# A hybrid encoder layer on eight cores: norms before the adaLN products, weights in 4 KB rows, the gate summed on VectorE, two buffers for normalized x

## The reference

```
mod = silu(c) @ w_ada + b_ada                     # (B, 3D)
shift, scale, gate = split(mod, 3)
h = rmsnorm(x, norm_g) * (1 + scale) + shift
a, ga, u, v, gb, ma, mb = split(h @ w_in, ...)    # 5 x 512, 2 x 1024 columns
y_a = (real 2-D DFT of a over (positions, 128 channels), mixed per group) * silu(ga)
y_b = (u * (w_s mixing layernorm(v) in chunks of 128 positions)) * silu(gb)
merged = sigmoid(ma) * (y_a @ w_pa) + sigmoid(mb) * (y_b @ w_pb)
y = rmsnorm(x + gate * (merged @ w_out), final_g)
```

## Time and profile before

| | |
|---|---|
| median of 3 runs | 1419.55 us (1417.86 to 1419.67) |
| profiled execution, its own time | 1415.01 us |
| its span on the slowest core (4); the others | 1413.5 us; 1406.5 to 1413.1 |
| granted TensorE clock, mean of each core | 0.953 to 0.959 |
| busy, core 4: TensorE, VectorE, ScalarE, GpSimd | 1245.9, 585.4, 503.5, 321.7 us |
| DMA | 48503 packets, 149.84 MB, 106 GB/s in the mean |

### The profile page before, as it was taken

How to read it: one execution, slowest core, us unless ns; L and a number is a source line. 1 busy time by engine, 2 the same in 40 slices (tenths; PEclk the granted TensorE clock), 3 DMA queues, 4 the chain that set the end, 5 groups by cost and what they waited for, 6 DMA issues and landing times.

```text
span 1413.5 us, 19855 instructions; the slowest of 8 cores (1406.5 to 1413.5 us)
## 1 busy us (share of the span) xinstructions
PE 1245.9 (88%) x6412; PEld 601.3 (43%) x6524; DVE 585.4 (41%) x956; ACT 503.5 (36%) x875; POOL 321.7 (23%) x398
## 2 busy tenths in 40 slices
PE   6476299699999997777996999999999699999997
PEld 1243144344444444443543444444444344444443
DVE  0353123344344445665433433444334334444344
ACT  0562213143332436664431334323343233333321
POOL 0000014413032130000145131321313613223122
PEclk9698699899999999999998999999999899999999
DMA  9899952122121255653521221212215112212111
GB/s 285 227 198 170 216 129 90 45 90 90 45 76 60 90 177 172 200 164 109 159 66 45 90 90 45 76 60 90 90 61 135 60 46 75 89 61 91 45 75 60
DMA packets 48503, 149.84 MB, mean 106 GB/s; under 512 B 5772, under 2 KB 18444, under 8 KB 45074
## 3 DMA queue, kind: packets, MB, share of 16 engines
q1 hardware_dynamic: 44514, 122.20, 25.4%
q0 software_dynamic: 2592, 17.96, 7.9%
q10 hardware_dynamic: 1296, 8.40, 1.9%
HBM read 135.03 MB, written 31.47 MB: 118 GB/s over the span
## 4 chain that ended last, share of the span: by engine, by line
PE 76%; DMA 8%; DVE 4%; issue 4%; ACT 4%; POOL 2%; SPq 1%; ACTq 0%; DVEq 0%; POOLq 0%
PE ps L652 41%; PE ps L610 12%; PE ps L743 6%; PE ps L737 6%; DMA Gd<-arena 5%; PE ps L662 5%; PE ps L498 2%; DMA arena<-w_ada 2%; ACT arena L442 2%; POOL arena L647 2%; PE ps L466 2%; ACT arena L479 1%; PE ps L820 1%; DMA arena<-Gd 1%; DVE arena L448 1%
## 5 line engine op out<-in xcount | busy, mean ns | idle before, releaser
L652 PE MATMUL ps<-arena 128*128 128x512 bf16 x2634 | 596.2, 380 | 7.1 <-DVE arena L692 3.7
L652 PEld LDWEIGHTS ps<-arena 128*128 128x128 bf16 x2688 | 262.4, 98 | 319.7 <-issue 8.0
L610 PE MATMUL ps<-arena 128*128 128x512 bf16 x734 | 173.9, 389 | 42.8 <-POOL arena L647 32.0
L729 ACT ACTIVATE arena<-ps 128x512 bf16<-128x512 f32 x192 | 113.2, 597 | 263.2 <-PE ps L652 259.7
L748 POOL TENSOR_TENSOR arena<-arena 128x512 bf16<-128x512 bf16 x96 | 125.1, 1303 | 283.3 <-DVE arena L746 283.3
L740 DVE TENSOR_TENSOR arena<-ps,arena 128x512 bf16<-128x512 f32 x96 | 66.4, 692 | 254.5 <-PE ps L737 254.5
L615 DVE TENSOR_TENSOR arena<-ps,arena 128x512 f32<-128x512 f32 x96 | 66.0, 691 | 189.7 <-PE ps L610 189.7
L610 PEld LDWEIGHTS ps<-arena 128*128 128x128 bf16 x768 | 75.9, 100 | 133.9 <-issue 50.1
L618 ACT ACTIVATE arena<-arena 128x1024 bf16<-128x1024 f32 x48 | 50.7, 1057 | 179.0 <-DVE arena L615 179.0
L442 ACT ACTIVATE arena<-arena 128x1024 bf16<-128x1024 f32 x96 | 100.5, 1047 | 6.1 <-DMA arena<-xB 5.9
L737 PE MATMUL ps<-arena 128*128 128x512 bf16 x384 | 98.6, 379 | 0.0
(11 more groups left out here) (79 smaller groups left out, 948.7 us busy)
## 6 DMA issues: line engine op xcount, KB each, us to landing
arena<-xB SPq DMA_DIRECT2D x96, 512.0 KB, 4.0
arena<-xA SPq DMA_DIRECT2D x48, 512.0 KB, 5.1
yu<-arena SPq DMA_DIRECT2D x48, 512.0 KB, 2.8
arena<-w_in POOLq DMA_DIRECT2D x9, 1024.0 KB, 19.4
arena<-w_ada ACTq DMA_DIRECT2D x8, 1024.0 KB, 19.7
Gd<-arena SPq DMA_DIRECT2D x48, 128.0 KB, 2.6
arena<-Gd SPq DMA_DIRECT2D x12, 512.0 KB, 6.9
arena<-w_out POOLq DMA_DIRECT2D x6, 1024.0 KB, 12.8
```

What stands on the lines that cost most here:

```text
L610: S.pe([lambda e, b=b, dmc=dmc, half=half: e.matmul(ps[b][:], lhsT=mg[:, dmc, j * 128:(j + 1) * 128], rhs=w_out_sb[:, dmc, half * 512:(hal ...
L652: S.pe([lambda e, kc=kc: e.matmul(ps[b][:], lhsT=w_in_sb[:, sec, kc, col:col + 128], rhs=hT0[:, kc, :], start=(kc == 0), stop=(kc == 7)) f ...
L729: S.op("act", lambda e, b=b, so=so: e.activation(out=bv(so, 512), in_=ps[b][:], func=AF.Sigmoid), reads=[("ps", b)], writes=gk(so, 1024))
```

## The change

Six things. (1) The norms: groups 0 and 1 of the first block are squared and scaled before the adaLN rows are copied out; the transposes of group 0 (`fe_t`) stand between the fifth and sixth piece of the adaLN products, the evictions with Gtab and modT (`fe_e`) after them. SP loads four chunks, the tables, and four more once the seventh piece of w_ada is there. (2) The weights lie in DRAM as blocks of 128 rows of 1024 float32, so that each partition's 16 KB come in four rows of 4 KB. (3) Normalized chunks have two buffers (`xoffs`), used by turns; the unused output of the squares goes to O_TYB. The ring of x chunks in A2 has 6 places instead of 8. (4) In both blocks chunks are normed in pairs: two squares, one root, one reciprocal, then the first chunk's scale on VectorE and the second's on GpSimd. (5) The gate: for each unit, `gate_acc` on VectorE multiplies each of the eight pieces with the condition's value per partition and adds them up, `gate_sum` sums over the partitions with a product with ones (float32, two of 512 columns) and adds the bias; gate_d and the three-row products are gone. The eight pieces and the bias are now loaded for each of the three units. (6) `gate_mul` runs on VectorE, and from other merge steps.

```diff
-    w_in = din("w_in", [9 * 128, 4096])
-    w_pa = din("w_pa", [128, 4096])
-    w_pb = din("w_pb", [128, 4096])
-    w_out = din("w_out", [128, 8192])
+    w_in = din("w_in", [9 * 512, 1024])
+    w_pa = din("w_pa", [512, 1024])
+    w_pb = din("w_pb", [512, 1024])
+    w_out = din("w_out", [1024, 1024])
...
+    def blocks(t, k):
+        return dram_ap(t, k * 512 * 1024, [[1024, 128], [128 * 1024, 4], [1, 1024]])
+
     def w_sec(s, after=()):
-        S.dma("pool", [lambda e: e.dma_start(
-            out=bv(O_WIN + 8192 * s, 4096), in_=w_in.ap()[s * 128:(s + 1) * 128, :])],
-            "s_w%d" % s, reads=after, writes=wink[s])
+        S.dma("pool", [lambda e: e.dma_start(out=bv(O_WIN + 8192 * s, 4096).rearrange("p (k n) -> p k n", k=4),
+                                             in_=blocks(w_in, s))], "s_w%d" % s, reads=after, writes=wink[s])
...
-    def x_sq(k, j, mode="pow"):
-        si = st_ctr[0] % 8
-        st_ctr[0] += 1
-        xk, sk = gk(XS[k], 4096), gk(O_XSR + 2048 * j, 2048)
-        S.op("act", lambda e: e.activation(out=xsr[:, j, :], in_=fv(XS[k], 1024), func=AF.Square, scale=0.03125,
-                                           accum_out=stat[:, si, 0:1]),
-             reads=xk, writes=sk + [("st", si)])
-        rstd(1, stat[:, si, 0:1], stat[:, si, 1:2], [("st", si)], [("st1", si)], mode)
-
-        def scale():
-            S.op("dve", lambda e: e.tensor_scalar(out=xsr[:, j, :], in0=fv(XS[k], 1024), scalar1=stat[:, si, 1:2],
-                                                  scalar2=None, op0=ALU.mult),
-                 reads=xk + [("st1", si)], writes=sk)
-        return scale
-
-    def x_norm(k, j, mode="pow"):
-        x_sq(k, j, mode)()
+    def stat2(n):
+        while st_ctr[0] % n:
+            st_ctr[0] += 1
+        si = st_ctr[0] % 16
+        st_ctr[0] += n
+        return si
+
+    def sq_op(k, si, junk, jk):
+        S.op("act", lambda e: e.activation(out=junk, in_=fv(XS[k], 1024), func=AF.Square, scale=0.03125,
+                                           accum_out=stat[:, 0, si:si + 1]),
+             reads=gk(XS[k], 4096), writes=jk + [("st", si)])
+
+    def scale_op(k, j, si, xoff, eng="dve"):
+        xr = bv(xoff + 2048 * j, 1024)
+        S.op(eng, lambda e: e.tensor_scalar(out=xr, in0=fv(XS[k], 1024), scalar1=stat[:, 1, si:si + 1],
+                                            scalar2=None, op0=ALU.mult),
+             reads=gk(XS[k], 4096) + [("st1", si)], writes=gk(xoff + 2048 * j, 2048))
+
+    def x_sq(k, j):
+        si = stat2(1)
+        sq_op(k, si, xsr[:, j, :], gk(O_XSR + 2048 * j, 2048))
+        rstd(1, stat[:, 0, si:si + 1], stat[:, 1, si:si + 1], [("st", si)], [("st1", si)], "pow")
+        return lambda: scale_op(k, j, si, O_XSR)
...
+    def gate_places(u):
+        return (XS[4], XS[5], [2, 3, 6, 7]) if u == 0 else (O_WIN, O_WIN + 4096, [2, 3])
+
+    def gate_w_load(u, kcs):
+        acc, gbc, ring = gate_places(u)
+        for kc in kcs:
+            k = ring[kc % len(ring)]
+            S.dma("sp", [lambda e, kc=kc, k=k: e.dma_start(out=fv(XS[k], 1024),
+                                                           in_=w_ada.ap()[kc * 128:(kc + 1) * 128, 2048:3072])],
+                  "s_x%d" % k, writes=gk(XS[k], 4096))
+
+    def gate_acc(u, kcs):
+        acc, gbc, ring = gate_places(u)
+        for kc in kcs:
+            k = ring[kc % len(ring)]
+            c = cs_sb[:, kc * 3 + u:kc * 3 + u + 1]
+            if kc == 0:
+                S.op("dve", lambda e, k=k, c=c: e.tensor_scalar(out=fv(acc, 1024), in0=fv(XS[k], 1024), scalar1=c,
+                                                                scalar2=None, op0=ALU.mult),
+                     reads=gk(XS[k], 4096) + ["cs"], writes=gk(acc, 4096))
+            else:
+                S.op("dve", lambda e, k=k, c=c: e.scalar_tensor_tensor(out=fv(acc, 1024), in0=fv(XS[k], 1024), scalar=c,
+                                                                       in1=fv(acc, 1024), op0=ALU.mult, op1=ALU.add),
+                     reads=gk(XS[k], 4096) + gk(acc, 4096) + ["cs"], writes=gk(acc, 4096))
+
+    def gate_bias(u):
+        acc, gbc, ring = gate_places(u)
+        S.dma("sp", [lambda e: e.dma_start(out=fv(gbc, 1024), in_=dram_ap(b_adaG, 0, [[0, 128], [1, D]]))],
+              "s_gb", writes=gk(gbc, 4096))
+
+    def gate_sum(u):
+        acc, gbc, ring = gate_places(u)
+        for h in range(2):
+            b = newbank()
+            S.pe([lambda e, b=b, h=h: e.matmul(ps[b][:], lhsT=ones_sb[:], rhs=fv(acc, 1024)[:, h * 512:(h + 1) * 512],
+                                               start=True, stop=True)], reads=["ones"] + gk(acc, 4096), writes=[("ps", b)])
+            gv, gkk = fv(gbc, 1024)[:, h * 512:(h + 1) * 512], gk(gbc + 2048 * h, 2048)
+            S.op("dve", lambda e, b=b, gv=gv: e.tensor_tensor(out=gv, in0=ps[b][:], in1=gv, op=ALU.add),
+                 reads=[("ps", b)] + gkk, writes=gkk)
+
+    def w_out_load():
+        S.dma("pool", [lambda e, k=k: e.dma_start(out=w_out_sb[:, 4 * k:4 * k + 4, :], in_=blocks(w_out, k))
+                       for k in range(2)], "s_wout", writes=woutk)
 
     def gate_mul(u, k):
-        off = gate_off(u)
+        acc, gbc, ring = gate_places(u)
         kk = gk(O_WOUT + 2048 * k, 2048)
-        S.op("pool", lambda e: e.tensor_tensor(out=w_out_sb[:, k, :], in0=w_out_sb[:, k, :], in1=fv(off, 1024), op=ALU.mult),
-             reads=kk + gk(off, 4096), writes=kk)
+        S.op("dve", lambda e: e.tensor_tensor(out=w_out_sb[:, k, :], in0=w_out_sb[:, k, :], in1=fv(gbc, 1024), op=ALU.mult),
+             reads=kk + gk(gbc, 4096), writes=kk)
...
-        def sq(self, g, j, mode="sqrt"):
-            i = 4 * g + j
-            self.load_to(i + 1)
-            self.sc.append((i, x_sq(self.ring[i % len(self.ring)], j, mode)))
-
-        def scales(self, n=1):
-            while len(self.sc) >= n:
-                i, fn = self.sc.pop(0)
-                fn()
-                self.load_to(i + 1 + len(self.ring))
+        def slot(self, g, j):
+            return self.ring[(4 * g + j) % len(self.ring)]
+
+        def sq(self, g, h, mode="sqrt"):
+            self.load_to(4 * g + 2 * h + 2)
+            si = stat2(2)
+            for j in (2 * h, 2 * h + 1):
+                sq_op(self.slot(g, j), si + j % 2, bv(O_TYB, 1024), gk(O_TYB, 2048))
+            rstd(2, stat[:, 0, si:si + 2], stat[:, 1, si:si + 2], [("st", si), ("st", si + 1)],
+                 [("st1", si), ("st1", si + 1)], mode)
+            for j in (2 * h, 2 * h + 1):
+                scale_op(self.slot(g, j), j, si + j % 2, self.xoffs[g % 2], ("dve", "pool")[j % 2])
+                self.load_to(4 * g + j + 1 + len(self.ring))
 
         def group(self, g):
-            for j in range(4):
-                self.sq(g, j)
-                self.scales(2)
-            self.scales()
+            self.sq(g, 0)
+            self.sq(g, 1)
...
-                    if q + 2 <= self.nq:
-                        self.sq(q + 2, j)
+                    if q + 2 <= self.nq and j % 2 == 0:
+                        self.sq(q + 2, j // 2)
                     st1 = a_proj(q, j, self.f, 4 * q + j, self.N1)
                     if self.pend:
                         self.pend.pop(0)()
                     self.pend.append(st1)
-                    self.scales(2)
-                self.scales()
...
+    S.op("act", lambda e: e.activation(out=cs_sb[:], in_=cT_sb[:], func=AF.Silu), reads=["cT"], writes=["cs"])
+
     A = ABlock(1, 4, list(range(8)), 16, lambda g: 0,
-               lambda i: rowsA(i) if i < 16 else rowsB(0, i - 16))
-    A.load_to(8)
+               lambda i: rowsA(i) if i < 16 else rowsB(0, i - 16), (O_XSR, O_Z + 16896))
+    A.load_to(4)
+    S.dma("sp", tabs[1:], "s_tab", writes=["tabs"])
+    tabs = []
+    A.load_to(8, after=gk(wada_off[6], 512))
     A.group(0)
-    A.fe(0)
     A.group(1)
+    mrow = fv(O_MROW, 2048)
+    mb = [newbank() for _ in range(4)]
+    for kc in range(8):
+        if kc == 5:
+            fe0 = fe_t(A.xoffs[0])
...
+        if t == 0:
+            gate_bias(u)
+            gate_w_load(u, range(4) if u == 0 else range(2))
         s3(0)
         silu_section(SEC["GB"], sgb, O_SGB)
+        if t == 0 and u:
+            gate_acc(u, (0, 1))
...
+            w_out_load()
+            if u:
+                gate_acc(u, (2, 3))
+                gate_w_load(u, (4, 5))
...
-            gate_rows()
-            gate_load(0)
+        if t == 0 and u:
+            gate_acc(u, (4, 5))
+            gate_w_load(u, (6, 7))
+        elif t == 0:
+            gate_acc(u, range(4))
+            gate_w_load(u, range(4, 8))
...
-            A2 = ABlock(0, 8, list(range(4, 12)), 32, lambda g: 1 if g == 8 else 1 + g // 4,
-                        lambda i: rowsA(16 + i) if i < 32 else rowsB(4, i - 32),
+            A2 = ABlock(0, 8, list(range(4, 10)), 32, lambda g: 1 if g == 8 else 1 + g // 4,
```

(16 more changed lines are left out.)

155 lines of the change are left out of this document (59 added, 96 removed).

## The result

| us | before | changed |
|---|---|---|
| median of the runs (lowest to highest, count) | 1419.61 (1417.86 to 1428.31, 4) | 1462.59 (1458.33 to 1502.79, 4) |
| ratio to before, 95% interval | | 1.0275 (1.0200 to 1.0351) |
| span of core 4 in the profiled execution | 1413.5 | 1436.6 |

A forecast was written before the change was run, and what follows sets the result against it. Bounds: TensorE's waits for x's scaling, GpSimd's gate products and the spectrum's load, with DMA nearly full in the first 175 us. Savings 45 + 14 + 11 = 70 from 1415.0 gave 1345 profiled; forecast 1348 us, range 1320 to 1380.

The forecast's parts named there:

- Opening, 10 us: Start of the kernel: first projection at 59 us instead of 68.9, bounds of the gain 5 and 14 us.
- GpSimd's half of group 0: Opening: TensorE's transposes start near 40 us, its last 24 adaLN passes end near 52, hidden by the wait for chunk 7.
- 4 KB rows: Front: shorter weight rows shorten queue turns and Fourier stores; spectrum's products at 125.5 us instead of 166.1, opening's 10 included.
- Stores of 3 to 5 us: Sign expected if the forecast held: Fourier stores landing in 3 to 5 us in the first 175 us.
- Late next is the load back: Loading the spectrum after the stores: 33 turns against weight rows, 8 us for each block.
- First unit, 92.5 us from spectrum to output: First gate unit: spectrum's products at 125.5 us, first output at 218 instead of 262.9; 45 us gained, front included.
- the 19 us of waits in that sum: First unit: 6 us for the fourth block, 5 for gate pieces, 4 for VectorE's products' tail, 4 for ScalarE's square.
- Units 1 and 2, 14 us: Later gate units: the 10.7 us wait for GpSimd falls away twice, less TensorE and VectorE costs; range 8 to 19.
- rival B: Gate: VectorE's sums become the new wait, first unit 15 us worse, the others' 14 us lost; 1377 us, chance 0.10.
- Second block, 11 us: Two buffers and pairs of chunks: one us per group, 4 ahead of group 1, 2 in output groups; range 5 to 17.
- rival C: Weight loads: writing the shorter weight rows becomes the limit and the kernel gets slower, 1436 us; chance 0.03.
- my two signs of being wrong: Weights landing later than the merge wants them, or ScalarE's squares holding the adaLN copies past 60 us.

The follow-up runs named there:

- fifth: Changed kernel with all scales on VectorE, and each pair's reciprocal and scales one step later, behind the projection's copies: ratio 0.9893 to before, median 1408.9 us.
- eighth: A combination: changed opening, 4 KB rows, two buffers, all scales on VectorE one step later, before's three-row gate with its products on VectorE: ratio 0.9766 to before.
- ninth: The eighth's kernel with five late weight loads held until the fourth block of the first spectrum load has landed: ratio 0.9631 to before, lowest 1366.5 us.
- tenth experiment: The fifth's kernel, units 1 and 2 loading only two gate pieces and summing these again for the other six (result incomplete): ratio 0.9811 to before.
- first experiment: Changed kernel with all of the A blocks' scales on VectorE, nothing else altered: ratio 1.0046 to before, median 1425.8 us.
- twelfth experiment: Also the last: changed kernel with five late weight loads held until the first spectrum load's fourth block has landed: ratio 1.0050 to before, median 1428.5 us.
- second experiment: Changed kernel with the weights again in rows of 16 KB, nothing else altered: ratio 1.0261 to before.
- eleventh experiment: The eighth's kernel with the odd chunks of the second A block scaled by GpSimd again: ratio 0.9970 to before.
- both series: The changed kernel's first runs, median 1462.59 us, and its repeat in the rounds of its variants, median 1463.8 us, ratio 1.0216 to before.
- the other seven: Fifth, eighth, ninth, tenth experiment, and the kernel before with only 4 KB rows (0.9941), the new gate (1.0088), or gate products on VectorE (0.9922).

## Why the prediction was wrong, point by point

- **Opening, 10 us: nearly right where GpSimd is left out.** With all scales on VectorE the first projection starts at 59.0 on core 4, the number forecast, but at 61.1 in the median of the eight cores, and at 62.5 to 62.7 in the fifth, eighth, ninth and tenth experiments, whose openings have no scale of GpSimd either. There chunk 7 decides: its square starts at 48.68 on core 4 of the first experiment and at 52.37 on core 2 of the fifth. The step that failed is "GpSimd's half of group 0 ... hidden by the wait for chunk 7": at 2.8 to 3.4 us a scale it isn't, the transposes stand ahead of 24 passes of TensorE, and ScalarE waits 3.24 us for these. The changed kernel gets 4.4. Not priced at all was what the scales do to GpSimd's own issues, which fall 22 us behind (twelfth experiment).
- **4 KB rows.** That short rows shorten the turns was right, and a turn's price nearly so (0.21 for 0.18). Stores of 3 to 5 us were wrong: 7.5. "Late next is the load back ... 8 us each" is the failed step. I had named the right place and undersized it: I left out that its issue waits 8 us for the last store, and that its 128 packets per engine (2 MB in rows of 1 KB) meet a backlog that before had drained by 160.63, where the first block landed in 5.26 us. In 160 to 170 us before's core 4 has of the two queues only

```profile
q1 hardware_dynamic: 1844, 1.96, 70.7%
```

  and the changed kernel's in 136 to 151 us, at its load,

```profile
q0 software_dynamic: 973, 1.93, 80.0%
q1 hardware_dynamic: 771, 0.98, 24.8%
```

  With the backlog held the spectrum starts at 126.3, against 125.5 forecast. The ninth and the twelfth experiment show this. It is worth 18 to 21 us at the combination's first output on the four cores that keep their clock, and at the changed kernel's, core by core on 4 to 7, 3.7, 11.0, 9.1 and 20.2.
- **First unit, 92.5 us from spectrum to output: right in sum, in part by luck.** It measures 92.2 with all scales on VectorE and 91.3 in the last experiment. But of the 19 us of waits in that sum, in the first experiment only 13.3 show, and others: none for the fourth block (6 forecast), 6.0 behind the gate's sums, and 7.3 for the tail that I took as 4 (a product takes VectorE 1.215 us, as priced). The rest of the 92.2 isn't traced. In the changed kernel the stretch is 101.4, with 7.3 us more of waits for later blocks of the load and 2.7 more for the gating.
- **Units 1 and 2, 14 us: products right (13.0), sums wrong.** "The sums lie beside projections that ScalarE evicts" failed. VectorE stands in order behind pieces whose two places its own earlier sums must free. On the changed kernel's core 4:

```profile
717.20 1.28 DVE L646 SCALAR_TENSOR_TENSOR arena<-arena,cs_sb 128x1024 f32<-128x1024 f32 x1 [5.12 <-DMA arena<-w_ada]
721.01 1.28 DVE L646 SCALAR_TENSOR_TENSOR arena<-arena,cs_sb 128x1024 f32<-128x1024 f32 x1 [2.53 <-DMA arena<-w_ada]
722.22 1.41 DVE L717 SCALAR_TENSOR_TENSOR arena<-ps,lng_sb,arena 128x512 bf16<-128x512 f32 x2
```

  and TensorE waits 9.6 us for L717. This was rival B, and the tenth experiment gives these waits 8.9 us in tile 4. Against it I had said that only the first unit has a weight backlog; but there, with four places, VectorE waits only 2.6 us for pieces (core 4, 150 to 250 us), and with two places it waits without a backlog.
- **Second block, 11 us: wrong in sign.** The changed kernel's block is 17.5 us longer. I priced the scales and not what the pair does to VectorE's order. I summed root, reciprocal and scales ahead of the transposes, and that was the wrong path: the projection's copies behind them are what TensorE waits for. GpSimd's price was above my upper bound of 2.13, by a third alone (2.84) and by 1.6 times beside VectorE (3.40), and was not even what decided in the block. It did decide ahead of it: of the 7.1 us before group 1, from which I took 4, TensorE waits 8.8 in the changed kernel. The Trainium skill's "SBUF — State Buffer", section "SBUF: two separate sides", calls the shared pair an exclusive lock, which spoke against the split; the rows above bear it out in part: beside VectorE's 0.76 us GpSimd's scale takes 3.40 instead of 2.84, 0.56 more.
- **The total.** 10.5 gained in front, then 1.5 given back before the second block, 17.5 in it, 7.2 and 7.4 in tile 4 and after: 23.1 us slower on core 4. Against the forecast of 70 us less that is 93 off: 34.5 in the front, 30.0 in and before the second block, 28.6 in the gate of units 1 and 2. I gave a slower kernel 0.03, and for another reason (rival C, out by the second experiment); of my two signs of being wrong neither came, for no weight was late and the adaLN copies did not wait for squares. The 20 us between core 4 and the slowest were in no case of mine. In 250 to 345 us core 0 has (stretch and length, busy us and count of TensorE, its weight loads, VectorE, ScalarE and GpSimd, then clock, DMA share, GB/s)

```profile
250.00:345.00 95.00, 89.41 (x378) 39.32 (x376) 39.77 (x54) 26.26 (x42) 18.24 (x23) 0.79 0.18 61
```

  and core 4

```profile
250.00:345.00 95.00, 91.03 (x450) 43.38 (x460) 41.66 (x63) 30.66 (x50) 22.97 (x31) 0.96 0.19 67
```

  with TensorE as busy and fewer matmuls done. What brings it stays open. It isn't bound to GpSimd's scales: in the eleventh experiment, whose front has none, core 6 has a mean clock of 0.930 and shows 0.83 in 180 to 250 us and its first output comes at 256.2 against 239.9 on core 0. Executions with a core at 0.94 or less are 9 of 10 for the changed kernel (both series), 9 of 10 for the eleventh experiment, 0 of 10 for the first, 0 of 4 for the second, 1 of 8 for the twelfth, 25 of 62 for the other seven, and 18 of 67 for the kernel before. So the change may make them likelier, but these counts come from different chips, and no experiment was made for it.

## What to carry to other kernels

On an engine that works in order, ask of each wait what stands behind it: here moving a reciprocal and two scales behind the copies that another engine needs was worth 21 us, seven times what the second buffer and the pairs gave in that block. When a change shortens the stage ahead, the next transfer meets a backlog it used to miss; price it in that backlog, and consider holding loads that are needed later: here TensorE waited for none of them, and it gave some 20 us where the clock held. A price taken between two bounds is no cover: where a step leans on it, ask what happens at a value beyond them.

## What the runs showed of the hardware

GpSimd scales 128x1024 float32 to bf16 in 2.84 us alone and 3.40 beside a scale of VectorE, about four times VectorE's 0.74, and longer than its own two-input product of that length in bf16 (2.13). Four load issues of 512 KB hold SP's queue for 9.81 us amid the weights and for 2.04 us with the weights held. TensorE's granted clock can have a mean of 0.79 on some cores for 165 us (180 to 345) while others doing the same work have 0.94 to 0.96; the output's 512-column products that start in it take 437 ns in the median there and 379 here.
